# The decay of an mLSTM in a fused two-block kernel: from products of ones in PSUM to rows sent to all partitions in SBUF

## The reference, cut to what matters

```
b = jnp.cumsum(lfc, axis=-1)
dmat = jnp.where(causal, b[..., :, None] - b[..., None, :] + lic[..., None, :], -jnp.inf)
...
s = jnp.einsum('bhtk,bhsk->bhts', qc, kc) * jnp.exp(dmat - m_t[..., None])
num = jnp.einsum('bhts,bhsv->bhtv', s, vc) + inter[..., None] * jnp.einsum('bhvk,bhtk->bhtv', c_st, qc)
den = jnp.sum(s, axis=-1) + inter * jnp.einsum('bhk,bhtk->bht', n_st, qc)
h = num / jnp.maximum(jnp.abs(den), jnp.exp(-m_t))[..., None]
```

## Time and profile before

| | |
|---|---|
| runs | 3218.23, 3220.1 and 3212.55 us, median 3218.23 |
| profiled execution | 3222.07 us, span 3220.3 |
| mean granted TensorE clock | 0.925 of full speed |
| busy over the span | PE 2843.7 us (88%), DVE 1816.1 (56%), ACT 1343.3 (42%), POOL 340.8 (11%) |
| the mLSTM's block | from 2207.6 to about 2316 us of the span |

### The profile page before, as it was taken

One profiled execution on the slowest core, in us unless ns is written; L12 is line 12 of the kernel. 1 busy time (PEld: TensorE's weight loads), 2 busy tenths in 40 slices (PEclk: granted clock), 3 DMA queues, 4 the chain that ended last, 5 costly groups with the idle time before them and its releaser, 6 DMA issues. The chain is left out here.

```text
span 3220.3 us, 42139 instructions
## 1 busy us (share of the span) xinstructions
PE 2843.7 (88%) x14427; PEld 2356.1 (73%) x14427; DVE 1816.1 (56%) x2255; ACT 1343.3 (42%) x2024; POOL 340.8 (11%) x230
## 2 busy tenths in 40 slices
PE   6999987799599999993999978578796999999997
PEld 5888766677578888882787767466675888887876
DVE  4995427754489999995362546664435333323344
ACT  4123427613178888883322133563335222221232
POOL 1222210010011111112222100002000000000000
PEclk9999998999799999996999977888598999999999
DMA  3112234133199999995122210302032111111122
GB/s 101 37 49 80 81 112 153 50 113 134 73 391 414 417 414 415 413 386 198 53 62 76 72 40 2 131 2 42 12 111 81 50 52 46 47 50 33 49 105 81
DMA packets 247659, 421.03 MB, mean 131 GB/s; under 512 B 33581, under 2 KB 152404, under 8 KB 247540
## 3 DMA queue, kind: packets, MB, share of 16 engines
q1 hardware_dynamic: 218356, 349.89, 29.9%
q10 hardware_dynamic: 20336, 39.59, 3.3%
q0 software_dynamic: 8848, 29.96, 2.8%
HBM read 349.05 MB, written 70.33 MB: 130 GB/s over the span
## 5 line engine op out<-in xcount | busy, mean ns | idle before, releaser
L2151 DVE TENSOR_TENSOR e_w_lo<-e_ring,e_w_hi 128x1024 fp32r<-128x1024 f32 x384 | 447.0, 1221 | 46.7 <-ACT e_w_hi L2078 46.7
L2078 ACT CAST e_w_hi<-e_ring 128x1024 fp32r<-128x1024 f32 x384 | 377.3, 1049 | 35.4 <-PE banks L2011 28.5
L2414 PE MATMUL banks<-h_hi,u_w_hi 128*128 128x512 f32 x672 | 261.5, 389 | 2.1 <-DVE u_w_lo L2457 2.1
L2415 PE MATMUL banks<-h_lo,u_w_hi 128*128 128x512 f32 x672 | 261.4, 389 | 0.0
L2416 PE MATMUL banks<-h_hi,u_w_lo 128*128 128x512 f32 x672 | 261.4, 389 | 0.0
L2009 PE MATMUL banks<-e_w_hi,e_xT_hi 128*128 128x512 f32 x512 | 203.1, 397 | 0.0
L2011 PE MATMUL banks<-e_w_hi,e_xT_lo 128*128 128x512 f32 x512 | 200.2, 391 | 0.0
L2010 PE MATMUL banks<-e_w_lo,e_xT_hi 128*128 128x512 f32 x512 | 199.8, 390 | 0.0
L937 DVE SCALAR_TENSOR_TENSOR conv<-x_first,vectors,conv 128x1024 f32<-128x1024 f32 x120 | 186.9, 1557 | 9.8 <-issue 0.9
L2414 PEld LDWEIGHTS banks<-h_hi,u_w_hi 128*128 128x128 f32 x672 | 126.1, 188 | 28.6 <-DVE u_w_lo L2457 2.5
L2268 PE MATMUL banks<-fd_w_hi,fd_s_hi 128*128 128x512 f32 x352 | 138.4, 393 | 9.6 <-DVE fd_s_lo L2327 8.8
(11 more groups left out here) (593 smaller groups left out, 6732.0 us busy)
## 6 DMA issues: line engine op xcount, KB each, us to landing
e_ring<-in_w_gate_e_dram SPq DMA_DIRECT2D x128, 512.0 KB, 6.1
e_ring<-in_w_up_e_dram SPq DMA_DIRECT2D x128, 512.0 KB, 6.1
e_ring<-in_w_down_e_dram SPq DMA_DIRECT2D x128, 512.0 KB, 5.2
yT<-in_ffn_w_up_dram SPq DMA_DIRECT2D x44, 512.0 KB, 3.8
expert_results<-nothing SPq DMA_DIRECT2D x1, 16384.0 KB
expert_results<-e_y ACTq DMA_DIRECT2D x32, 512.0 KB, 7.6
p_w<-in_w_in_dram SPq DMA_DIRECT2D x24, 512.0 KB, 3.7
fd_w<-in_ffn_w_down_dram SPq DMA_DIRECT2D x44, 256.0 KB, 2.5
```

Source lines behind the costliest of these rows:

```text
L2078: nc.scalar.copy(w_hi[:, part, :], experts.ring[:, slot, :]).then_inc(w_rounded, 1)
L2151: tt(w_lo[:, part, :], experts.ring[:, slot, :], w_hi[:, part, :].bitcast(F32), ALU.subtract).then_inc(w_split, 1)
L2414: nc.tensor.matmul(bank, w_hi[:, up, k, :], h_hi[:, k, tokens], start=(k == 0), stop=False)
L2415: nc.tensor.matmul(bank, w_hi[:, up, k, :], h_lo[:, k, tokens], start=False, stop=False)
```

## The change

The products of ones and the masking products go. SP sends the high and the low row of rise(t) of a head to all 128 partitions, into two buffers of plain f32, `rise` and `masked`. DVE's new `raise_rows` adds the two into `rise` and writes `rise` plus the mask of each key tile into `masked`. ACT takes its exponentials from these in SBUF; for a crossing chunk it does the first 128 columns from `masked` and the others from `rise`, in two instructions. It no longer waits for TensorE's scores; DVE's `mix` does. The three banks of the decay are free, and the score ring and `w` have four places.

```diff
-    loads = 16 * 9
+    loads, RING = 16 * 8, 4
...
     def score_bank(c, n):
-        return K.ps[:, c % 3, 0:n]
-
-    def decay_bank(c, n):
-        return K.ps[:, 3 + c % 3, 0:n]
+        return K.ps[:, c % RING, 0:n]
...
+        @block.sync
+        def _(sp):
+            for h in range(HM):
+                x = h % 2
+                if h >= 2:
+                    sp.wait_ge(exped, NC * (h - 1))
+                for part, dst in enumerate((rise, masked)):
+                    sp.dma_start(dst[:, x, :], R["rise"][h, part:part + 1, :].to_broadcast([P, S])).then_inc(rise_landed[x], 16)
...
-                if h == 0:
-                    pool.wait_ge(filled, 1)
-                pool.dma_start(rise[0:2, x, :], R["rise"][h:h + 1].rearrange("o c s -> (o c) s")).then_inc(loaded[x], 16)
...
-                    crossing = q0 == j * P
-                    mm(score_bank(c, n), k[:, x, keys], q[:, x, q0:q0 + n], start=True, stop=True)
-                    last = mm(decay_bank(c, n), ones[:], rise[:, x, q0:q0 + n], start=True, stop=not crossing)
-                    if crossing:
-                        last = mm(decay_bank(c, P), K.ident_r[:], K.causal_t_r[:], start=False, stop=True)
-                    last.then_inc(scored, 1)
+                    mm(score_bank(c, n), k[:, x, keys], q[:, x, q0:q0 + n], start=True, stop=True).then_inc(scored, 1)
...
-                    pe.wait_ge(mixed, i * (2 * NC) + (NC * x + c + 4))
+                    pe.wait_ge(mixed, i * (2 * NC) + (NC * x + c + RING + 1))
...
-                    act.wait_ge(scored, i * (2 * NC) + (NC * x + c + 2 * NC + 1))
+                    if c == 0:
+                        act.wait_ge(risen, i * 2 + (x + 1))
+                    act.wait_ge(mixed, i * (2 * NC) + (NC * x + c + 1))
                     act.sem_inc(begun, 1)
-                    nc.scalar.activation(w[:, c % 3, 0:n], decay_bank(c, n), ACT.Exp,
-                                         bias=K.mlstm_keys[:, bass.ds(i * 2 + (4 * j + x), 1)]).then_inc(exped, 1)
+                    bias = K.mlstm_keys[:, bass.ds(i * 2 + (4 * j + x), 1)]
+                    crossing = P if q0 == j * P else 0
+                    if crossing:
+                        last = nc.scalar.activation(w[:, c % RING, 0:P], masked[:, x, q0:q0 + P], ACT.Exp, bias=bias)
+                    if n > crossing:
+                        last = nc.scalar.activation(w[:, c % RING, crossing:n], rise[:, x, q0 + crossing:q0 + n], ACT.Exp, bias=bias)
+                    last.then_inc(exped, 1)
...
-            nc.vector.tensor_copy(ones[:], K.const("ones"))
-            nc.vector.tensor_scalar(rise[:], K.const("ones")[:, 0:1].unsqueeze(2).to_broadcast([P, 2, S]), 0.0, None, ALU.mult)
...
+            def raise_rows(i, x):
+
+                dve.wait_ge(rise_landed[x], i * 32 + 32)
+                nc.vector.tensor_tensor(rise[:, x, :], rise[:, x, :], masked[:, x, :], ALU.add)
+                dve.drain()
+                nc.vector.tensor_tensor(masked[:, x, :].rearrange("p (t n) -> p t n", n=P), rise[:, x, :].rearrange("p (t n) -> p t n", n=P),
+                                        K.const("causal_t").unsqueeze(1).to_broadcast([P, NT, P]), ALU.add).then_inc(risen, 1)
...
             def mix(i, x, chunks):
                 for c, j, q0, n in chunks:
                     half = 0 if c < 4 else 1
+                    dve.wait_ge(scored, i * (2 * NC) + (NC * x + c + 2 * NC + 1))
                     dve.wait_ge(exped, i * (2 * NC) + (NC * x + c + 1))
...
                 if more:
+                    raise_rows(*following(i, x))
                     mix(*following(i, x), early[0:1])
...
+            raise_rows(0, 0)
             mix(0, 0, chunks_of(0))
```

More of the change, by code:

```diff
@@ L2783, in mlstm_attention @@
         ("filled", "staged", "scored", "exped", "mixed", "weighed", "rated", "stored", "fetching", "begun"))
+    rise_landed, risen = [K.sem(f"{tag}_rise_landed{b}") for b in range(2)], K.sem(f"{tag}_risen")
     o_turned, o_kept = K.sem(f"{tag}_o_turned"), K.sem(f"{tag}_o_kept")
     def score_bank(c, n):
-        return K.ps[:, c % 3, 0:n]
-    def decay_bank(c, n):
-        return K.ps[:, 3 + c % 3, 0:n]
+        return K.ps[:, c % RING, 0:n]
     def chunks_of(half):
@@ L2808, in mlstm_attention @@
         k = K.sb(scope, f"{tag}_k", [P, 2, S], F32R)
-        rise = K.sb(scope, f"{tag}_rise", [P, 2, S], F32R)
-        ones = K.sb(scope, f"{tag}_ones", [P, P], F32R)
-        w = K.sb(scope, f"{tag}_w", [P, 3, HALF])
+        rise, masked = (K.sb(scope, f"{tag}_{n}", [P, 2, S]) for n in ("rise", "masked"))
+        w = K.sb(scope, f"{tag}_w", [P, RING, HALF])
         weights = [K.sb(scope, f"{tag}_weights{h}", [P, 4 * (h + 1), HALF]) for h in range(2)]
@@ L2920, in _ @@
             nc.vector.memset(vs[:, :, :, DV:DV + 1], 1.0)
[L2921 to L2922 removed]
             dve.drain()
             dve.sem_inc(filled, 1)
[L2925 removed]
+            dve.sem_inc(mixed, RING)
             dve.wait_ge(o_turned, 1)
             nc.vector.tensor_copy(turned_to[:, 1, :], K.ps[:, 6:8, :].rearrange("p c n -> p (c n)")).then_inc(o_kept, 1)
+            def raise_rows(i, x):
[4 more added lines that the diff above has]
+                                        K.const("causal_t").unsqueeze(1).to_broadcast([P, NT, P]), ALU.add).then_inc(risen, 1)
             def mix(i, x, chunks):
@@ L2931, in mix @@
                     half = 0 if c < 4 else 1
+                    dve.wait_ge(scored, i * (2 * NC) + (NC * x + c + 2 * NC + 1))
                     dve.wait_ge(exped, i * (2 * NC) + (NC * x + c + 1))
-                    nc.vector.tensor_tensor(weights[half][:, j, HALF - n:HALF], w[:, c % 3, 0:n], score_bank(c, n),
+                    nc.vector.tensor_tensor(weights[half][:, j, HALF - n:HALF], w[:, c % RING, 0:n], score_bank(c, n),
                                             ALU.mult).then_inc(mixed, 1)
```

## The result

The changed kernel takes 3228.86 us (median of 9 runs, 3224.98 to 3233.94) against 3220.1 for the kernel before in the same session (9 runs, 3212.55 to 3225.63). The ratio is 1.0028, with a 95% interval of 1.0017 to 1.0038: slower, by 5.5 to 12.2 us. The forecast was 3216.6, no difference, and its range ended at 3227. The profiled execution took 3228.86 us, span 3227.0, mean granted clock 0.918.

A forecast was written before the change was run, and what follows sets the result against it. It took a ring of ACT and DVE to bound each head up to its third finish, then TensorE at 1.2 GHz. Heads together -2.1 us, waits +0.5, start 0: -1.6 us, so 3216.6 us; range 3208 to 3227.

The forecast's parts named there:

- Up to 1.5 us of delay of q and k beside SP's traffic is covered by the raising: Start of head 0: q and k may land up to 1.5 us later at no cost, behind DVE's two additions.
- 0 for the start: First exponential of head 0 stays where it was, near 2217.5 us; bounds -2.0 and +3.9 us.
- 5.73 behind the first exponential: Head 0's first finish: 2.4 us of early exponentials, then 1.23, 0.71 and 1.38; before it was 7.66 us.
- three signs of being wrong: Last leg under 13.5 us, additions taking 2 us, or split instructions costing 0.4 us each.
- estimate of 6.8 us: Start: landing of the first pair of rows with 1 MB of q and k mixed in, from the skill page.
- Last leg, 14.6 us: Third to last finish of a head: 14.6 us against 14.71, TensorE's 1.7 us saving spent waiting for the mask.
- Second and third leg, +0.55: First to third finish of a head: split exponentials and longer sources add 0.55 us, 5.78 against 5.23.
- +0.5 set aside for DVE's waits: Some 30 mixes in the chain wait for two semaphores instead of one: +0.5 us, bounds 0 and 2.
- First leg, 3.53: Previous head's last finish to a head's first: 3.53 us against 4.39.
- TensorE staying at 1.2 GHz "I cost at nothing": First three legs of a head: a lower clock costs nothing, 7.1 us of work beside a ring of 9.3.
- Rival 1: Faster: cheap raising, split instructions vanishing in the pipeline and an early first pair give -9.5 us, 3208.7 us; chance 0.14.
- Rival 2: Slower: DVE's additions decide the head; both at 2.4 us give +5.6 us, 3224 us; chance 0.14.

The follow-up runs named there:

- h1_late: Changed kernel with SP's row transfers for head 1 sent only after head 0's first score; ratio to the kernel before 1.0008.
- spread_start: spread with GpSimd's q and k of head 1 also held until head 0's first score; ratio to the kernel before 0.9991.
- placed_sp: placed with head 0's q and k issued by SP behind its rows, head 1's held until head 0's first score; ratio to the kernel before 0.9998.
- halves: Changed kernel with rows sent and added in halves of 512 columns, head 1's rows after head 0's q and k landed; ratio to the kernel before 1.0011.
- spread_whole: spread with each crossing chunk's exponential in one instruction from the masked rows (output differs); executed once, no ratio, last finish 1.94 us earlier.
- spread_dup: spread with each late score product made twice, the first into a bank nobody reads; ratio to the kernel before 0.9995.
- old_rows: Kernel before with the change's four row transfers sent by SP at the block's start into SBUF nobody reads; ratio to the kernel before 1.0011.
- placed: spread with additions for tiles 0-3 behind row shares of tiles 1 and 2, tiles 4-7 behind 5 and 6; ratio to the kernel before 0.9998.
- spread: Changed kernel with head 1's rows sent after head 0's first score, additions in three pieces behind row shares 0 to 2; ratio to the kernel before 0.9995.
- change_dup_all: Changed kernel with products nobody reads in the places of the decay and masking products; ratio to the kernel before 1.0030.

## Why the prediction was wrong, step by step

- **The step that failed: "Up to 1.5 us of delay of q and k beside SP's traffic is covered by the raising", and with it the sum's "0 for the start".** The delay was 6.79 us. The first exponential was forecast within 0.6 us, but scores came at 2223.12, 6.2 us behind it. The forecast first finish, 5.73 behind the first exponential, is at +13.41; measured +18.09. That is 4.7 us of a miss of 7.5 in the stage (5.95 against -1.6). Runs put 4.35 of the delay on head 1's rows (h1_late; 3.2 to 4.6 over all profiles) and leave 2.4 for head 0's own. For that, spread_start and placed_sp exclude head 1's q and k and GpSimd's queue, and the records of h1_late show GpSimd's first bytes behind SP's; no run leaves head 0's rows out. The prediction had costed the transfers that it was looking at, whose first pair was there at 2213.98 (forecast 2215.0), and took for the others, which so far had landed in 3 us, that they still would. Its three signs of being wrong were all about the raising, the split and the last leg, and none of them appeared.
- **What the engines share.** The Trainium skill says that transfers of SP and GpSimd run on the same sixteen engines and interleave ("DMA: Bandwidth & Descriptors", section "Issuing engines are not separate DMA queues"). The traces agree: GpSimd's queue falls from 0.2 MB a us to 0.07 to 0.10 beside SP's in halves, and the issuer makes no difference in placed_sp. The prediction's estimate of 6.8 us came from the Trainium skill's fit (the same page, section "Anatomy of one DMA"), which is given there for single transfers of GpSimd. It came close for the first pair of rows, which was there 6.4 us behind 2207.6. For q and k, which it counted in, it was far off: the first product started 15.5 us behind 2207.6, with 4.2 MB asked for and not 2 MB, and 231 to 233 GB/s and not 436. The measurement decides.
- **Last leg, 14.6 us: mechanism right, size off.** The additions stand in the chain (1.21 and 1.29 us, forecast 1.22) and TensorE stalls for finish 4 (1.72 us on its weight loads, 1.46 on its products, in head 1). The leg was 15.46, 15.11, 15.48. Hidden, it is 13.32 (forecast 13.0). So the raising costs 2.0 us a head, 6.1 in all, where the sum had 1.6 and 4.8. The leg term was 2.2 us too small over three heads.
- **Second and third leg, +0.55: 0.71 measured, 0.92 in head 3.** The split is 0.50 of it (spread_whole), near the 0.57 costed; the remaining 0.21, or 0.8 us over four heads, may be the +0.5 set aside for DVE's waits, which no run took by themselves.
- **First leg, 3.53: right** (3.61, 3.65, 3.60).
- **TensorE staying at 1.2 GHz "I cost at nothing": right** in the legs where the high stretch used to be (spread_dup). What the clock can be worth where TensorE is the bound is shown by one profile of old_rows, 5.2 us in a leg.
- **Rival 1** needed three lucky costs; none came. **Rival 2, raising decides (3224 us)**, is not what happened: the additions took 1.2 to 1.3 us, not 2.4. The larger part of the slower outcome came from the start, for which the prediction had a bound of +3.9 us on the rows and none on q and k.

**Left open.** The timed differences lie up to 5 us above the stage's in nearly all kernels (halves: ratio 1.0011, 0.6 to 6.4 us more than before, with a stage that is 1.26 shorter). Most intervals allow for it, those of halves and placed don't, and that of placed_sp just doesn't. In the profiles of halves and placed the part behind the stage is 2.5 and 2.0 us longer than in the first profile of the kernel before, and 1.3 and 0.8 longer than in its second; whether the change has to do with that wasn't found. For this reason no version counts as faster than the kernel before: spread, spread_start and placed can't be told from it in time, though their stages are 2.8 to 4.2 us shorter. Why old_rows was granted 2.4 GHz for over 20 us and change_dup_all for 7 wasn't settled. Neither was the 2.4 us of delay that is left with head 0's rows in front, other than by exclusion and by the order of the bytes.

## What to carry to other kernels

When a change adds transfers at a point where others are already in flight, price what it does to those others: list who waits for each, add up the bytes asked for in the same microseconds, and hold back everything that isn't needed soon. And a unit of work that is moved to an idle-looking engine goes into the gaps of its chain, in pieces behind the instructions that free it, not in front of the one that everybody waits for: here the same additions cost 6.1 us in one place and nothing that the legs show in another.

## What the runs showed of the hardware that was not expected

- Loads of 128 KB to 32 partitions that landed in 3.0 to 3.4 us (medians of four) took 9.6 to 11.0 us beside 2 MB of rows sent to all partitions, at 231 to 233 GB/s together. By the transfer records, GpSimd's loads alone moved 0.20 to 0.25 MB in most microseconds, and rows in SP's queue up to 0.42 (spread). Which engine issued q and k made no difference to the first product (+8.57 against +8.88).
- In one profile of old_rows a late start paid for itself by the clock: TensorE stood idle for 12.4 us, had 1.2 GHz for the first microseconds of work, was then granted 2.4 GHz through head 0's last leg, and ended 0.63 us late, not 6.14. The changed kernel stood idle for 13.1 us and had no such stretch, so the idle time alone doesn't bring it.
- A granted clock of 0.84 in place of 0.50 over head 2's first three legs, with the late scores made twice, left these legs within 0.05 us (spread_dup): in a stretch that waits for other engines a higher granted clock made nothing shorter.
- An ACT exponential of 128 columns from SBUF takes 0.39 us, one of 512 0.71; three additional instructions in two legs cost 0.50 us.
